# Gate and up of a float32r expert block: one 512-column matmul for the high and low halves of the tokens

## What is computed

```python
def expert_choice_ffn(x, w_router, w_gate, w_up, w_down):
    tok = x.reshape(n_tok, D)                                    # 1024 tokens of one group
    aff = jax.nn.softmax((tok @ w_router).astype(jnp.float32), axis=-1)
    gate, idx = lax.top_k(aff.T, cap)                            # cap = 128 tokens per expert and group
    xe = jnp.take(tok, idx, axis=0)
    h = jax.nn.silu(jnp.einsum('ecd,edf->ecf', xe, w_gate)) * jnp.einsum('ecd,edf->ecf', xe, w_up)
    ye = jnp.einsum('ecf,efd->ecd', h, w_down) * gate[..., None].astype(x.dtype)
    out = jnp.zeros_like(tok).at[idx.reshape(-1)].add(ye.reshape(-1, D))
```

## Time and profile before

| | us |
|---|---|
| median of three runs | 3321.15 |
| lowest and highest | 3319.88, 3324.86 |
| the profiled execution, span from first to last instruction | 3317.6 |
| TensorE busy in it | 3111.9 (94%) |
| VectorE busy | 1891.1 (57%) |
| ScalarE busy | 1357.6 (41%) |

### The profile page before, as it was taken

The page is one execution under the profiler, slowest core; times in us unless marked ns, Lnnn a source line. Parts: engine busy times, 40 slices in busy tenths (PEclk is TensorE's granted clock), DMA queues, the critical chain, the costliest instruction groups (busy, mean ns, idle before and its releaser), DMA issues.

```text
span 3317.6 us, 54591 instructions
## 1 busy us (share of the span) xinstructions
PE 3111.9 (94%) x21544; PEld 2878.0 (87%) x21544; DVE 1891.1 (57%) x2257; ACT 1357.6 (41%) x1668; POOL 477.4 (14%) x387
## 2 busy tenths in 40 slices
PE   7998999989958999999999999999999999999990
PEld 7997888968848998998989989899898999989990
DVE  6545777856664555555545555555555555555546
ACT  3216777861113334333334343333434333343423
POOL 2543232401120000010010000100010010110005
PEclk9999999999979999999999999999999999999995
DMA  6331101013344566565565655656566565665535
GB/s 203 124 100 49 33 9 30 33 62 121 116 165 133 201 200 204 191 191 202 193 206 190 199 191 191 206 200 197 191 197 203 195 191 198 202 193 202 180 126 215
DMA packets 367271, 533.68 MB, mean 161 GB/s; under 512 B 32592, under 2 KB 307792, under 8 KB 367056
## 3 DMA queue, kind: packets, MB, share of 16 engines
q1 hardware_dynamic: 352464, 488.48, 43.8%
q0 software_dynamic: 10368, 37.75, 4.4%
q10 hardware_dynamic: 4224, 4.19, 0.4%
HBM read 469.57 MB, written 60.82 MB: 160 GB/s over the span
## 4 chain that ended last, share of the span: by engine, by line
issue 66%; PE 18%; DMA 5%; POOLq 4%; POOL 3%; DVE 2%; DVEq 1%; ACT 1%; SPq 0%; ACTq 0%
PE ps_o L747 5%; DMA acc_d<-ysb,idx_s 4%; PE ps_pv L683 4%; PE ps_t L672 3%; PE ps_s L637 2%; PE ps_s L638 2%; POOLq L1585 1%; PE ps_l L764 1%; POOLq L1462 1%; POOLq L1470 1%; POOL qkv L1476 1%; PE ps_m L692 1%; POOLq L1576 1%; POOL w_l L1568 1%; PE ps_m L623 1%
## 5 line engine op out<-in xcount | busy, mean ns | idle before, releaser
L838 PE MATMUL ps_gu<-x_h,w_h 128*128 128x256 f32 x4096 | 1160.5, 283 | 20.0 <-issue 18.5
L838 PE MATMUL ps_gu<-x_h,w_l 128*128 128x256 f32 x4096 | 1159.1, 283 | 0.0
L838 PE MATMUL ps_gu<-x_l,w_h 128*128 128x256 f32 x4096 | 1159.1, 283 | 0.0
L1338 DVE TENSOR_TENSOR w_l<-w_raw,w_h 128x2048 fp32r<-128x2048 f32 x380 | 859.4, 2290 | 288.0 <-ACT w_h L1076 288.0
L838 PEld LDWEIGHTS ps_gu<-x_h,w_h 128*128 128x128 f32 x4096 | 786.3, 192 | 25.8 <-issue 23.9
L1076 ACT ACTIVATE w_h<-w_raw 128x2048 fp32r<-128x2048 f32 x384 | 719.3, 1907 | 195.5 <-PE ps_y L853 186.3
L838 PEld LDWEIGHTS ps_gu<-x_l,w_h 128*128 128x128 f32 x4096 | 786.3, 192 | 0.1
L838 PEld LDWEIGHTS ps_gu<-x_h,w_l 128*128 128x128 f32 x4096 | 786.3, 192 | 0.0
L1101 ACT ACTIVATE sg<-ps_gu 128x256 f32<-128x256 f32 x256 | 98.1, 383 | 941.9 <-PE ps_gu L838 941.9
L1389 DVE TENSOR_TENSOR hf<-sg,ps_gu 128x256 f32<-128x256 f32 x256 | 107.1, 418 | 578.4 <-ACT sg L1101 578.4
L853 PE MATMUL ps_y<-w_h,hh 128*128 128x512 f32 x1024 | 321.5, 395 | 0.0
(11 more groups left out here) (193 smaller groups left out, 3909.6 us busy)
## 6 DMA issues: line engine op xcount, KB each, us to landing
w_raw<-in_w_gate SPq DMA_DIRECT2D x128, 1024.0 KB, 5.3
w_raw<-in_w_up SPq DMA_DIRECT2D x128, 1024.0 KB, 6.1
w_raw<-in_w_down SPq DMA_DIRECT2D x128, 1024.0 KB, 6.0
xin<-in_x SPq DMA_DIRECT2D x16, 512.0 KB, 5.9
xln_d<-xln SPq DMA_DIRECT2D x16, 512.0 KB, 5.5
res<-xln_d SPq DMA_DIRECT2D x16, 512.0 KB, 3.2
h_d<-hid SPq DMA_DIRECT2D x16, 512.0 KB, 2.6
acc_d<-acc SPq DMA_DIRECT2D x16, 512.0 KB, 2.6
```

Source lines behind the costliest of these rows:

```text
L838: last = nc.tensor.matmul(ps_gu[n % 3][:, u, :], w[:, k, cols], a[:, k, :], start=k == 0 and q == 0, stop=k == KD - 1 and q == 2)
L1338: nc.vector.tensor_tensor(w_l[:, c % RING, :], w_raw[:, c % RING, :], w_h[:, c % RING, :].bitcast(f32), ALU.subtract).then_inc(w_lo, 1)
```

## The change

- `x_h` and `x_l` become one tensor `x_hl` in which, for each slice of the width, the 256 columns of the high half stand beside the 256 of the low.
- For each `k` and `u` there are two matmuls in place of three: `w_h` by both halves (512 columns, L840 of the kernel after) and `w_l` by the high half (256 columns, L842). The 512 columns fill a bank: the products by the low half of the tokens stand in its second half and no longer add up with the rest in PSUM.
- A block so takes two banks, gate and up. There are two sets of two banks (before: three single banks), and `ps_x` is no bank of its own any more: the transposes of the next expert's tokens go through the `ps_gu` banks during the down rounds, behind a wait for all of `h_split`.
- ScalarE copies the second halves of both banks to SBUF (`by_xl`, 512 columns, L1103), VectorE adds them to the first halves (`pre`, 512 columns, L1393), ScalarE takes silu of `pre` (L1107) and VectorE multiplies `sg` by `pre` (L1398).
- TensorE waits at block `n` for `pre_ready` of block `n-2`.
- ScalarE and VectorE take up the chunks one for each block: behind silu of block `n`, chunk `n+3` (for `n` from 1), and chunk 19 at the end, in place of two behind each odd block.

```diff
-        x_h = sb("x_h", [P, KD, C2], f32r)
-        x_l = sb("x_l", [P, KD, C2], f32r)
+        x_hl = sb("x_hl", [P, KD, 2, C2], f32r)
+        by_xl = sb("by_xl", [P, 2, 2, C2])
+        pre = sb("pre", [P, 2, 2, C2])
-        ps_gu = [pb(f"ps_gu{i}", [P, 2, C2]) for i in range(3)]
+        ps_gu = [pb(f"ps_gu{i}", [P, 2, 2, C2]) for i in range(2)]
-        ps_x = pb("ps_x", [P, 4, P])
+        ps_x = ps_gu[0][:, 0, :, :].rearrange("p h (k t) -> p (h k) t", t=P)
 # TensorE, x_round
                 if not start:
-                    pe.wait_ge(x_lo, XR * e + n)
+                    pe.wait_ge(h_split, KF * e)
 # TensorE, stage_e
                     if n % 2 == 0:
                         pe.wait_ge(w_lo, NCHUNK * e + n + 2)
-                    if not (first and n < 3):
-                        pe.wait_ge(h_split, KF * e + n - 2)
+                    if not (first and n < 2):
+                        pe.wait_ge(pre_ready, KF * e + n - 1)
                     for u in range(2):
                         for k in range(KD):
-                            for q, (w, a) in enumerate(((wh, x_h), (wh, x_l), (wl, x_h))):
-                                last = nc.tensor.matmul(ps_gu[n % 3][:, u, :], w[:, k, cols], a[:, k, :],
-                                                        start=k == 0 and q == 0, stop=k == KD - 1 and q == 2)
+                            both = ps_gu[n % 2][:, u, :, :].rearrange("p h t -> p (h t)")
+                            nc.tensor.matmul(both, wh[:, k, cols], x_hl[:, k, :, :].rearrange("p h t -> p (h t)"),
+                                             start=k == 0, stop=False)
+                            last = nc.tensor.matmul(both[:, 0:C2], wl[:, k, cols], x_hl[:, k, 0, :],
+                                                    start=False, stop=k == KD - 1)
                     last.then_inc(gu_done, 1)
 # ScalarE, stage_e
-                for j in range(KF // 2):
-                    for n in (2 * j, 2 * j + 1):
-                        act.wait_ge(gu_done, KF * e + n + 1)
-                        if not (first and n < 2):
-                            act.wait_ge(h_split, KF * e + n - 1)
-                        nc.scalar.activation(sg[:, n % 2, :], ps_gu[n % 3][:, 0, :], ACT.Silu).then_inc(silu_done, 1)
-                    for c in (2 * j + RING, 2 * j + RING + 1):
-                        w_hi_copy(e, c, False)
+                for n in range(KF):
+                    act.wait_ge(gu_done, KF * e + n + 1)
+                    nc.scalar.activation(by_xl[:, n % 2, :, :], ps_gu[n % 2][:, :, 1, :], ACT.Copy).then_inc(xl_copied, 1)
+                    act.wait_ge(pre_ready, KF * e + n + 1)
+                    if not (first and n < 2):
+                        act.wait_ge(h_split, KF * e + n - 1)
+                    nc.scalar.activation(sg[:, n % 2, :], pre[:, n % 2, 0, :], ACT.Silu).then_inc(silu_done, 1)
+                    if n:
+                        w_hi_copy(e, n - 1 + RING, False)
+                w_hi_copy(e, KF - 1 + RING, False)
 # VectorE, stage_e
+                for n in range(KF):
+                    dve.wait_ge(xl_copied, KF * e + n + 1)
+                    nc.vector.tensor_tensor(pre[:, n % 2, :, :], by_xl[:, n % 2, :, :], ps_gu[n % 2][:, :, 0, :],
+                                            ALU.add).then_inc(pre_ready, 1)
+                    dve.wait_ge(silu_done, KF * e + n + 1)
...
+                    if n:
+                        w_lo_sub(e, n - 1 + RING)
+                w_lo_sub(e, KF - 1 + RING)
```

More of the change, by code:

```diff
@@ L252, in encoder_layer @@
         gu_done, silu_done, h_split = sem("gu_done"), sem("silu_done"), sem("h_split")
+        xl_copied, pre_ready = sem("xl_copied"), sem("pre_ready")
         dn_done, y_ready = sem("dn_done"), sem("y_ready")
@@ L279, in x_bank @@
             if not start:
-                return ps_x[:, :, :]
+                return ps_gu[n // 2][:, n % 2, :, :].rearrange("p h (k t) -> p (h k) t", t=P)
             return ps_y[n // 2][:, (n % 2) * 512:(n % 2 + 1) * 512].rearrange("p (k t) -> p k t", t=P)
@@ L1089, in x_hi_copy @@
                 act.wait_ge(xt_d, XR * e + n + 1)
-                nc.scalar.activation(x_h[:, 4 * r:4 * r + 4, g * CAP:(g + 1) * CAP], x_bank(n, start), ACT.Copy).then_inc(x_hi, 1)
+                nc.scalar.activation(x_hl[:, 4 * r:4 * r + 4, 0, g * CAP:(g + 1) * CAP], x_bank(n, start),
+                                     ACT.Copy).then_inc(x_hi, 1)
             for n in range(XR):
@@ L1376, in x_lo_sub @@
                 dve.wait_ge(x_hi, XR * e + n + 1)
-                dst = (slice(None), slice(4 * r, 4 * r + 4), slice(g * CAP, (g + 1) * CAP))
-                nc.vector.tensor_tensor(x_l[dst], x_bank(n, start), x_h[dst].bitcast(f32), ALU.subtract).then_inc(x_lo, 1)
+                x_h, x_l = (x_hl[:, 4 * r:4 * r + 4, lo, g * CAP:(g + 1) * CAP] for lo in range(2))
+                nc.vector.tensor_tensor(x_l, x_bank(n, start), x_h.bitcast(f32), ALU.subtract).then_inc(x_lo, 1)
             for n in range(XR):
@@ L1383, in stage_e @@
             def stage_e(e, first, last_e):
[L1384 to L1396, removed]
+                for n in range(KF):
[3 more added lines that the diff above has]
+                    dve.wait_ge(silu_done, KF * e + n + 1)
+                    if n == 0 and not first:
+                        dve.wait_ge(dn_done, (KF // 2) * e)
+                    nc.vector.tensor_tensor(hf[:, n % 2, :], sg[:, n % 2, :], pre[:, n % 2, 1, :], ALU.mult)
+                    dve.drain()
+                    nc.vector.tensor_copy(hh[:, n, :], hf[:, n % 2, :])
+                    dve.drain()
+                    nc.vector.tensor_tensor(hl[:, n, :], hf[:, n % 2, :], hh[:, n, :].bitcast(f32),
+                                            ALU.subtract).then_inc(h_split, 1)
+                    if n:
+                        w_lo_sub(e, n - 1 + RING)
+                w_lo_sub(e, KF - 1 + RING)
                 for m in range(KF // 2):
```

## The result

The kernel after takes 3333.0 us (median of 7 runs, 3329.8 to 3334.9) against 3321.2 before (also 7 runs): 1.0032 times as long, with a 95% interval of 1.0021 to 1.0042. The forecast was 3333.8. The time came out, but not the sum: its term for the merge was twice too large, and a gain that it did not have made up for most of that.

A forecast was written before the change was run, and what follows sets the result against it. TensorE's matmul stream was taken to bound the kernel. Per expert, 3.58 us gained by the merge against 4.38 lost to stalls made 12.7 us more over 16 experts, 3333.8 us in all, range 3300 to 3365.

The forecast's parts named there:

- The bound: Whole kernel: TensorE, busy 94% of the span, sets the end; other engines count only if later than TensorE needs them.
- The moved chunk: Gate and up: an odd chunk is taken up half a pair later, so only block `n-1`, 5.54 us, covers it.
- the chain: From the last matmul of block `n-2` through copy, addition, silu, `w_h` and `w_l` to TensorE: 5.97 us together.
- The term of 0.73 us: TensorE's stall at blocks 4, 6, 8, 10, 12 and 14 of each expert: 0.73 us each, 4.38 us an expert.
- The merge: Gate and up matmuls: one in three removed, a block 5.54 us in place of 5.76, 0.224 us gained for each.
- rows 7 and 8: Profile rows timing 512-column matmuls: eight at 0.226 us each, and 0.23 where a 256 follows; the forecast took 0.226.
- a pair at 0.360: Rival, merge gives less: a pair takes 0.360 not 0.346, a block stays at 5.76 us, 3369 us; chance 0.08.
- The term of 57 us: The merge's gain over all 256 blocks, 0.224 us each: 57.3 us if TensorE never waits.
- The sum: Per expert 3.58 us gained, 4.38 lost; 12.7 us more over 16 experts, 3333.8 us in all; chance 0.62.
- What costs nothing: `pre_ready` waits, additions behind `w_l` (cover 0.3 us), raw chunks (13 us early) and down-round transposes were to hold up nothing.
- The signs in the profile: Expected after: 96 TensorE waits for `w_l`, 0.6 to 0.7 us each, block pairs 11.8 us, VectorE 177 us busier, ScalarE 153.
- the cover holds: Rival: chain at most 5.37 us, no even block waits, all 57.3 us gained, 3263.9 us; chance 0.16 wholly or in part.

The follow-up runs named there:

- the one with two chunks: Kernel after, with ScalarE and VectorE again taking up two chunks behind each odd block; no wait for `w_l` left: 3271.6 us, 0.9845 of before.
- two edits: Kernel after, with two chunks behind each odd block again (3271.6 us), or one chunk per block copied ahead of silu and subtracted ahead of the product (3272.3 us).

## Why the prediction was right

By its steps:
- **The bound.** Right: TensorE's stream sets the end and ScalarE and VectorE count where they come later than it needs them.
- **The moved chunk.** Right in place, number and size. The waits fell on 6 even blocks of each of 16 experts and nowhere else; the chain was 6.07 us in place of 5.97, of which 0.05 lies at the silu (0.33 to `w_h` in place of 0.28) and 0.08 ahead of TensorE (0.13 in place of 0.05; the forecast had 0.03 for the register instruction outside the chain). The term of 0.73 us, 70 us in all, measured 62 us (the kernel after less the one with two chunks). The chain is longer than summed, but a block of 5.65 us covers more than one of 5.54: most waits cost 0.69, and all 96 together 68. Most of the other 6 came back from blocks that ran at 5.55 in the kernel after and at 5.65 in the one with two chunks.
- **The merge.** The step "rows 7 and 8 agree on 0.226, and I take it" failed. In strict turn a pair costs 0.353 us, not 0.346, and a block mostly 5.65 us; the forecast 5.55 was met by 67 of the 256 blocks alone. The term of 57 us was worth 27 (256 × 0.107) in the kernel without waits. Rows 7 and 8 show each width in rows of its own and one change between them; the prediction said so, gave 0.08 to a pair at 0.360, and had nothing for the values between. The rule of the Trainium skill (TensorE: Matmul & The Clock Gate, Back-to-back issue gap), a fixed part of 2.5 ns and by estimate 10 us in all, was off by 17 us on the other side, less than the 30 of the rows. It did not come nearer for its own reason, since with 512 and 256 columns in longer rows a pair takes 0.348, 12 ns below three matmuls of 0.120.
- **The turn of the loop.** Not in the prediction. Its pause was read in the row of 13 waits at "issue", 18.5 us, and taken as given, though the change takes 256 of 976 matmuls out of the loop's body. Removing it gave 13 × 1.5 to 1.6, some 20 us.
- **The sum.** Forecast: -57 + 70 = 13 us more. Measured: -27 - 20 + 62 = 15, against 12 between the medians. The time was hit because 30 us too much credit for the merge met 20 us of an unseen gain and 8 us too much for the stall. That is luck: the forecast's 0.62 was not given for errors that cancel.
- **What costs nothing.** Right: `pre_ready`, the late addition, the raw chunks and the transposes held nobody.
- **The signs in the profile.** The 96 waits, their places and the granted clock came as forecast (1.00 in the window from 1318 to 1457). Two blocks with a wait are 11.9 to 12.0 us apart in place of 11.8, and VectorE and ScalarE are 195 and 166 us busier in place of 177 and 153. `w_l` and `w_h` add 9 and 11 us of that, `silu` from SBUF 9.

The rival "the cover holds" became true in two edits, at 3272 us rather than at the 3264 that was priced for it.

## What to carry to other kernels

Before a step is put onto the way between two matmul blocks, add up the whole queue behind it: here the copy and addition were cheap and covered, and so was the new order of the chunks, and only both together came to more than one block. Moving the same work two queue places, with no instruction less, was worth 1.8%; with two chunks behind each odd block and the matmuls in twos the kernel runs in 3251 us, 2.1% below the one before. When a loop's body gets longer or shorter, read the engine's wait at the turn of the loop and the instruction queue's transfers: they can appear and vanish as a whole.

## What the runs showed of the hardware that was not expected

- TensorE's pause of 1.5 us at each turn of a loop with 976 matmuls in its body, with 182 transfers (2.98 MB) in the instruction queue, and none with 848 or fewer (62 or 59 transfers, 1.0 MB).
- Matmuls of 512 and 256 columns in strict turn take mostly 0.353 us a pair and in some stretches 0.347, in twos 0.348, in eights 0.349.
- A row of 512 columns starts at 0.228 to 0.236 us a matmul for the first five and settles at 0.226, behind 256 columns in gate and up and at the start of the down rounds alike.
- A `silu` that reads SBUF takes 420 ns where from PSUM it took 383, and the next instruction starts 0.33 us behind its start in place of 0.28. The Trainium skill (VectorE: DVE Perf Modes, section on the TRN2 errata) gives ScalarE a fixed cost of 224 cycles from SBUF and 172 from PSUM; the 52 between them are, as an estimate, 0.043 us, and the trace agrees, with 0.037.
